# Two small loads move from SyncE's queue to ScalarE's, ahead of a two-stack transformer kernel

## The chip, the cores and the metric
The kernel runs on one core of a Trainium2 chip. The metric is the device time of one launch in microseconds (us), the median of several runs. The profile is of one further execution; its times count from the start of its span.

## What is computed
The reference runs x, 512 tokens of 1024 float32 values, through two layers of one kind (differential attention, a gated unit and dilated attention side by side, each fed by one wide projection, merged through gates) and then two of another kind (four kinds of attention side by side and a gated feed-forward part). Each layer of the first kind begins with an RMS norm, and that is all the change is near:
```python
def rmsnorm(t, g):
    tf = t.astype(jnp.float32)
    y = tf * lax.rsqrt(jnp.mean(tf * tf, axis=-1, keepdims=True) + EPS)
    return (y * g.astype(jnp.float32)).astype(t.dtype)

def hybrid_layer(x, ...):
    h = rmsnorm(x, norm_g)
    proj = jnp.einsum('bsd,dc->bsc', h, w_in)
    ...
```
So nothing of a layer can be computed before x, the factors norm_g and the first columns of w_in are on the chip.

## The kernel before
**Products.** Every weight matrix is cut into units of 128 x 1024 values (512 KB). SyncE loads them in the order of use into a ring of raw buffers. ScalarE rounds each to a high part (w_hi, line 1285), and VectorE subtracts to get the low part (w_lo, line 1302). TensorE multiplies in three products, high by high, low by high and high by low (lines 667 to 669). Each engine has its own program, written out by hand in order, and the engines meet at semaphores. A later load waits until TensorE has finished with the unit whose buffer it takes (`unit_done`, in `load`).

**The start.** x comes in four blocks of 128 tokens, 512 KB each. For a block, ScalarE makes the sum of squares and from it one factor per token (`rms`, lines 622 to 624; its results are in `small`). VectorE multiplies the block by this factor and by the gain row (`rms_scale`, line 630, into hn). TensorE transposes hn with the help of an identity matrix (line 601). ScalarE and VectorE take high and low part of the transposed block (h_hi line 609, h_lo line 615). Then the first products begin.

**The gain row.** norm_g is needed on every partition as a row of 1024 values, and it is in memory with 8 values on each of 128 partitions (`colp[:, 0:P1_SUBLN]`, 4 KB in all). VectorE waits for the identity (line 2000, `ident_loaded`) and then for these factors (line 1316, `norm_loaded`), and multiplies the one by the other in two halves of 128 x 512 (`gain_diagonal`, line 1318, gain_diag). TensorE multiplies each half by a matrix of ones, which sums over the partitions (`gain_sums`, line 1312), and VectorE copies the sums to gain_row (line 1913). The identity is 128 x 128 values, 64 KB (`const[:, 0:P]`).

**TensorE until then.** Its program begins with two products of zeros, one of 512 and one of 256 columns (line 1340), which wait only for a VectorE memset. Behind them it waits for the identity and then for gain_diag:
```python
pe.wait_ge(zeros_ready, 1)
zero_products(1)
zero_products(1, SEQ // 2)
pe.wait_ge(ident_loaded, 16)
gain_sums(pe)
entry_transpose(pe, e, 0, hn[0], (0,))
zero_products(2)
v_block(0, 0)
```

**The order of work.** VectorE: gain_diag twice, gain_row's first half, hn of block 0, w_lo of unit 0, h_lo, the high part of unit 1 (line 1924), hn of block 1, w_lo of unit 1, gain_row's second half. ScalarE: a load of its function table (line 1628), the statistics of block 0, w_hi of unit 0, h_hi of block 0, the statistics of block 1, and so on. SyncE: the identity (line 1104), the factors (line 1105), then x's blocks (line 1107) and the first four weight units (line 1073) in turns, then the remaining parameters, tables and masks (lines 1112 to 1119), one after the other with no wait among them.

Of the kernel before, what the change touches and what calls it, by code (L numbers as in the profile page):

```python
# [37 lines left out]
P = 128  # L38
# [64 lines left out]
P1_NORM, P1_SUBLN, P1_LAM, P1_INIT, P1_KEEP = 0, 8, 9, 9 + 4 * HD, 10 + 4 * HD  # L103
# [52 lines left out]
def program(nc, x_in, pos_in, const_in, mask_in, swa_in, rope2_in, col_in, w_in, row1_in,  # L156
            row2_in, out):
    ctx = ExitStack()
    with ctx:
# [4 lines left out]
        def sb(name, shape, dt=F32, at=None):  # L164

            size = 4
            for s in shape[1:]:
                size *= s
            offset = top[0] if at is None else at
            addr[name] = offset  # L170
            if at is None:
                top[0] += (size + 31) // 32 * 32
            return nc.alloc_sbuf_tensor_at(name, shape, dt, offset=offset)
# [3 lines left out]
        def sem(name):  # L177
            made = ctx.enter_context(nc.semaphore(name))
            names[made.num] = name
            return made  # L180
# [42 lines left out]
        const = sb("const", [P, C_KEEP])  # L223
        colp = sb("colp", [P, COLS])
# [106 lines left out]
        ident_loaded = sem("ident_loaded")  # L331
        params_loaded = sem("params_loaded")
        cols_loaded = sem("cols_loaded")
        norm_loaded = sem("norm_loaded")
# [298 lines left out]
        def ln_stat(act, st, i, tb):  # L633

            act.wait_ge(ln_centre, NB * i + tb + 1)
            st.wait(st(nc.scalar.activation(junk[:, :], x[:, tb, :], ACT.Square, bias=small[:, 52 + tb:53 + tb],
                                            accum_out=small[:, 16 + tb:17 + tb])))
            st.wait(st(nc.scalar.activation(small[:, 20 + tb:21 + tb], small[:, 16 + tb:17 + tb], ACT.Ln,
                                            scale=1.0 / D, bias=LN_EPS)))
            nc.scalar.activation(small[:, 20 + tb:21 + tb], small[:, 20 + tb:21 + tb], ACT.Exp, scale=-0.5) \  # L640
              .then_inc(ln_ready, 1)

        def ln_gain(st, i, tb):

            return st(nc.vector.scalar_tensor_tensor(out=hn[tb][:, :], in0=x[:, tb, :], scalar=small[:, 52 + tb:53 + tb],
                                                     in1=ln_row[:, 0:D], op0=ALU.add, op1=ALU.mult))

        def ln_scale(dve, i, tb, cols=slice(0, D)):

            dve.wait_ge(ln_ready, NB * i + tb + 1)  # L650
            return nc.vector.scalar_tensor_tensor(out=x[:, tb, cols], in0=hn[tb][:, cols], scalar=small[:, 20 + tb:21 + tb],
                                                  in1=ln_row[:, D:2 * D][:, cols], op0=ALU.mult, op1=ALU.add)
# [407 lines left out]
        def sync_program(sp):  # L1060
# [40 lines left out]
                sp.wait_ge(unit_done, first_unit(DEPTH + layer) + B2_END + i + 1)  # L1101
                sp.dma_start(raw_of(n), w_in[stored_at(n), :, :]).then_inc(last_loaded[i], 16)

            sp.dma_start(const[:, 0:P], const_in[:, 0:P]).then_inc(ident_loaded, 16)
            sp.dma_start(colp[:, 0:P1_SUBLN], col_in[0, :, 0:P1_SUBLN]).then_inc(norm_loaded, 16)
            for tb in range(NB):
                sp.dma_start(x[:, tb, :], x_in[tb * P:(tb + 1) * P, :]).then_inc(x_loaded[tb], 16)
                if tb < 2:
# [160 lines left out]
        def cast_to(act, n):  # L1269


            for u in range(cast_units[0], min(n, UNITS - 1) + 1):
                if u in EXTRA:
                    e, i = EXTRA[u]
                    if EXTRA_TURN[u] == extras_cast[0]:
                        cast_extra(act, e)
                elif u in TURN:
                    act.wait_ge(raw_loaded[TURN[u] % RAW], 16 * loaded_parts(u))
                    if u in STEP_OF and STEP_OF[u][2] == 1:
                        act.wait_ge(pair_sums, 4 * (PAIR_STEPS * STEP_OF[u][0] + STEP_OF[u][1]) + 2)  # L1280
                    if u in KR_UNITS:
                        nc.scalar.activation(by_tile(hi_of(u))[:, :, kr_high], by_tile(raw_of(u))[:, :, kr_high], ACT.Copy) \
                          .then_inc(hi_cast, 1)
                    else:
                        nc.scalar.activation(hi_of(u), raw_of(u), ACT.Copy).then_inc(hi_cast, 1)  # L1285
                cast_units[0] = u + 1

        def split_to(dve, n):


            for u in range(split_units[0], min(n, UNITS - 1) + 1):
                if u in EXTRA:
                    if EXTRA_TURN[u] == extras_split[0]:
                        split_extra(dve, *EXTRA[u])
                elif u in TURN:
                    dve.wait_ge(hi_cast, TURN[u] + 1)
                    if u in KR_UNITS:
                        high = by_tile(hi_of(u))
                        nc.vector.tensor_tensor(high[:, :, kr_low], by_tile(raw_of(u))[:, :, kr_high], high[:, :, kr_high].bitcast(F32),
                                                ALU.subtract).then_inc(split_done, 1)  # L1300
                    else:
                        nc.vector.tensor_tensor(lo_of(u), raw_of(u), hi_of(u).bitcast(F32), ALU.subtract) \  # L1302
                          .then_inc(split_done, 1)
                split_units[0] = u + 1
# [1696 lines left out]
        def last_down(dve, layer):  # L3001


            at, n_end = Counts(names, DEPTH + layer), first_unit(DEPTH + layer + 1)

            def one(tb, between=None):
                for c in range(2):
                    residual_sum(dve, at(tok_ready, 2 * (NB - 1) + tb + c), n_end - LAST_UNITS // 2 * (1 - c), c, 1.0, tb, True,
                                 LAST_BANKS[c])
                    if between and c == 0:  # L3010
                        between(tb - 1)
                centre(dve, at(tok_out, 2 * NB + 2 * tb + 2), tb)
                dve.wait_ge(ln_centre, NB * LN2[layer] + tb + 1)
            return one
# [423 lines left out]
        with nc.Block() as block:  # L3438
            @block.sync
            def _(sp):  # L3440
                sync_program(sp)

            @block.tensor
            def _(pe):
                for layer in range(DEPTH):
                    tensor_block1(pe, layer)
                for layer in range(DEPTH):
                    tensor_block2(pe, layer)

            @block.scalar  # L3450
            def _(act):
                st = Steps(act, act_step)
                for layer in range(DEPTH):
                    scalar_block1(act, st, layer)
                for layer in range(DEPTH):
                    scalar_block2(act, st, layer)
                nc.scalar.preload_act_table_set("natural_log_exp_and_others")
                cast_to(act, UNITS - 1)
                for tb in range(NB):
                    ln_stat(act, st, LN2[-1], tb)  # L3460
                act.wait_ge(final_ready, NB + 1)
                act.dma_start(out[(NB - 1) * P:NB * P, SEQ:D], x[:, NB - 1, SEQ:D]).then_inc(stored, 16)

            @block.vector
            def _(dve):
                st = Steps(dve, dve_step)
                for layer in range(DEPTH):
                    vector_block1(dve, st, layer)
                for layer in range(DEPTH):
                    vector_block2(dve, st, layer)  # L3470
                split_to(dve, UNITS - 1)
                i, residual = LN2[-1], last_down(dve, DEPTH - 1)
                dve.wait_ge(ln_rows_loaded, 16 * (i + 1))
                gained = {}

                def finish(tb):
                    st.wait(gained[tb])
                    ln_scale(dve, i, tb).then_inc(final_ready, 1)

                for tb in range(NB):  # L3480
                    residual(tb, finish if tb else None)
                    gained[tb] = ln_gain(st, i, tb)
                st.wait(gained[NB - 1])
                for c in range(2):
                    ln_scale(dve, i, NB - 1, slice(c * SEQ, (c + 1) * SEQ)).then_inc(final_ready, 1)
# [165 lines left out]
```

## Time and profile before
| | us |
|---|---|
| median of 3 runs (2294.7 to 2295.55) | 2294.81 |
| the profiled execution | 2294.94 |
| its span | 2293.1 |
| TensorE busy | 2279.9 |
| VectorE busy | 1618.4 |
| ScalarE busy | 1046.4 |

The clock that TensorE was granted over the span was 0.999 of full speed. PE is TensorE's matmuls and PEld its weight loads, DVE is VectorE, ACT is ScalarE, SP is SyncE; SPq and ACTq are the issues of transfers on these engines. A row of an operation gives output and inputs by the names in the program, their shapes, and, in square brackets, how long the engine stood idle before it and what it waited for.

### The profile page before, as it was taken

What the parts mean: (1) busy time and instruction counts of PE and PEld (TensorE: products, weight loads), DVE (VectorE), ACT (ScalarE), POOL (GpSimd) and SP (SyncE); (2) the same over time, 40 slices, a digit from 0 to 9 for tenths busy, and PEclk for the clock granted to TensorE, in tenths of its full rate; (3) what the DMA queues carried; (4) which work ended last, traced back from release to release, by engine and by line L of the source; (5) the groups of instructions that cost most, each with busy time, mean ns of one, the idle gap of its engine ahead of it and who ended that gap; (6) DMA issues with size and microseconds to landing.
All of it is one profiled execution on the core that took longest, in us unless ns stands there. A gap on an engine that the chain in (4) does not pass through costs nothing.

```text
span 2293.1 us, 31916 instructions
## 1 busy us (share of the span) xinstructions
PE 2279.9 (99%) x12048; PEld 1892.9 (83%) x12048; DVE 1618.4 (71%) x3021; ACT 1046.4 (46%) x1972; POOL 0.2 (0%) x4
## 2 busy tenths in 40 slices
PE   9999999999999999999999999999999999999998
PEld 7888888998888888998877788888887768888887
DVE  6788768775578777875677768567567786668565
ACT  5456544443446554443567533223246764223222
POOL 0000000000000000000000000000000000000000
PEclk9999999999999999999999999999999999999999
DMA  5343333343343333334231242424303113422422
GB/s 177 105 111 105 98 78 115 107 143 101 129 118 106 106 95 109 102 102 156 69 89 56 66 140 74 138 65 129 129 29 102 47 47 104 146 92 81 134 65 96
DMA packets 81624, 232.67 MB, mean 101 GB/s; under 512 B 16000, under 2 KB 16896, under 8 KB 80704
## 3 DMA queue, kind: packets, MB, share of 16 engines
q1 hardware_dynamic: 81328, 230.37, 32.6%
q8 instruction: 97, 1.59, 0.3%
q14 instruction: 55, 0.45, 0.1%
q10 hardware_dynamic: 144, 0.26, 0.0%
HBM read 208.96 MB, written 4.20 MB: 93 GB/s over the span
## 4 chain that ended last, share of the span: by engine, by line
PE 98%; DVE 1%; ACT 0%; issue 0%; DMA 0%; DVEq 0%; SPq 0%
PE bank L667 24%; PE bank L669 23%; PE bank L668 23%; PE bank L1593 3%; PE bank L1592 3%; PE bank L1591 3%; PE bank L2676 2%; PE bank L2677 2%; PE bank L2678 2%; PE bank L1454 2%; PE bank L1438 1%; PE bank L2459 1%; PE bank L2491 1%; PE bank L2475 1%; PE bank L601 1%; PE bank L1427 1%
## 5 line engine op out<-in xcount | busy, mean ns | idle before, releaser
L667 PE MATMUL bank<-h_hi,w_hi 128*128 128x512 f32 x1680 | 666.1, 396 | 0.2
L669 PE MATMUL bank<-h_lo,w_hi 128*128 128x512 f32 x1680 | 655.0, 390 | 0.0
L668 PE MATMUL bank<-h_hi,w_lo 128*128 128x512 f32 x1680 | 654.8, 390 | 0.0
L1302 DVE TENSOR_TENSOR w_lo<-raw_w,w_hi 128x1024 fp32r<-128x1024 f32 x294 | 355.8, 1221 | 79.3 <-ACT w_hi L1285 76.9
L1285 ACT ACTIVATE w_hi<-raw_w 128x1024 fp32r<-128x1024 f32 x293 | 307.6, 1054 | 180.1 <-DMA raw_w<-w_dram 172.3
L667 PEld LDWEIGHTS bank<-h_hi,w_hi 128*128 128x128 f32 x1680 | 315.7, 188 | 69.8 <-issue 8.6
L669 PEld LDWEIGHTS bank<-h_lo,w_hi 128*128 128x128 f32 x1680 | 315.4, 188 | 67.4
L668 PEld LDWEIGHTS bank<-h_hi,w_lo 128*128 128x128 f32 x1680 | 315.9, 188 | 60.3
L2923 ACT ACTIVATE nrm<-bank 128x512 f32<-128x512 f32 x44 | 26.3, 598 | 286.4 <-PE bank L669 286.4
L3337 DVE TENSOR_TENSOR ytmp<-nrm,bank 128x512 f32<-128x512 f32 x26 | 17.9, 687 | 117.0 <-PE bank L669 116.9
L1757 ACT ACTIVATE prob<-prob,small 128x128 f32<-128x128 f32 (+3 forms) x128 | 70.8, 556 | 61.5 <-DVE small L893 61.5
L2676 PE MATMUL bank<-seven_hi,y_hi 128*128 128x512 f32 x252 | 98.0, 389 | 0.0
L2677 PE MATMUL bank<-seven_hi,y_lo 128*128 128x512 f32 x252 | 98.0, 389 | 0.0
L1845 ACT ACTIVATE ext<-bank 128x256 f32<-128x256 f32 x72 | 27.6, 383 | 130.9 <-PE bank L1593 130.1
L3337 DVE TENSOR_TENSOR y_raw<-nrm,bank 128x512 f32<-128x512 f32 x18 | 12.4, 687 | 91.5 <-PE bank L669 91.5
L3405 DVE SCALAR_TENSOR_TENSOR x<-x,bank 128x512 f32<-128x512 f32 x84 | 54.8, 682 | 20.7 <-PE bank L2678 20.7
L1772 ACT ACTIVATE pT<-bank 128x384 f32<-128x384 f32 (+3 forms) x84 | 36.8, 470 | 61.4 <-PE bank L1438 61.3
L893 DVE CUSTOM_DVE_ANT_0 prob<-bank,causal 128x128 f32<-128x128 f32 (+3 forms) x96 | 43.2, 487 | 29.3 <-PE bank L1427 20.3
L2937 ACT ACTIVATE seven_hi<-sum_raw 128x512 fp32r<-128x512 f32 x54 | 31.2, 621 | 56.4 <-PE bank L2678 56.4
L667 PE MATMUL bank<-act_hi,proj_hi 128*128 128x512 f32 x144 | 56.3, 391 | 0.0
L668 PE MATMUL bank<-act_hi,proj_lo 128*128 128x512 f32 x144 | 56.2, 391 | 0.0
L2678 PE MATMUL bank<-down_lo,y_hi 128*128 128x512 f32 x144 | 56.0, 389 | 0.0
(456 smaller groups left out, 4576.4 us busy)
## 6 DMA issues: line engine op xcount, KB each, us to landing
raw_w<-w_dram SPq DMA_DIRECT2D x276, 512.0 KB, 3.6
down_raw<-w_dram SPq DMA_DIRECT2D x36, 512.0 KB, 4.5
raw_w<-w_dram SPq DMA_DIRECT2D x36, 256.0 KB, 3.0
proj_raw<-w_dram SPq DMA_DIRECT2D x36, 256.0 KB, 2.9
extra_raw<-w_dram SPq DMA_DIRECT2D x10, 512.0 KB, 4.7
x<-x_dram SPq DMA_DIRECT2D x8, 512.0 KB, 6.4
k_lo<-k_lo SPq DMA_DIRECT2D x32, 128.0 KB, 2.3
ln_row<-row_dram SPq DMA_DIRECT2D x4, 1024.0 KB, 6.6
```

The source lines that it names most:

```text
L667: nc.tensor.matmul(dst, lh, rh, start=start, stop=False)
L668: nc.tensor.matmul(dst, ll, rh, start=False, stop=False)
L669: return nc.tensor.matmul(dst, lh, rl, start=False, stop=stop)
L1285: nc.scalar.activation(hi_of(u), raw_of(u), ACT.Copy).then_inc(hi_cast, 1)
L1302: nc.vector.tensor_tensor(lo_of(u), raw_of(u), hi_of(u).bitcast(F32), ALU.subtract) \
L1591: nc.tensor.matmul(to, high[:, w], m_hi, start=begin, stop=False, skip_group_check=True)
L1592: nc.tensor.matmul(to, low[:, w], m_hi, start=False, stop=False, skip_group_check=True)
L1593: made = nc.tensor.matmul(to, high[:, w], m_lo, start=False, stop=k == 3, skip_group_check=True)
L1757: nc.scalar.activation(prob[m][:, own], prob[m][:, own], ACT.Exp, scale=-1.0, bias=small[:, 24 + 2 * qb + m:25 + 2 * qb + m], accum_out=sm ...
L2676: nc.tensor.matmul(bank[t][:, :], y_hi[:, p, a, y], high, start=begin, stop=False, skip_group_check=True)
L2677: nc.tensor.matmul(bank[t][:, :], y_lo[:, p, a, y], high, start=False, stop=False, skip_group_check=True)
L2678: made = nc.tensor.matmul(bank[t][:, :], y_hi[:, p, a, y], low, start=False, stop=p == PAIRS - 1, skip_group_check=True)
```

## The change
The two first issues of SyncE's program are taken out. ScalarE's program begins with them, in the other order: the factors first, then the identity. SyncE's program now begins with x's first block. The semaphores that the two transfers raise, and who waits for them, stay as they are.
```diff
@@ sync_program
-            sp.dma_start(const[:, 0:P], const_in[:, 0:P]).then_inc(ident_loaded, 16)
-            sp.dma_start(colp[:, 0:P1_SUBLN], col_in[0, :, 0:P1_SUBLN]).then_inc(norm_loaded, 16)
             for tb in range(NB):
                 sp.dma_start(x[:, tb, :], x_in[tb * P:(tb + 1) * P, :]).then_inc(x_loaded[tb], 16)
                 if tb < 2:
@@ the program of ScalarE
                 st = Steps(act, act_step)
+                act.dma_start(colp[:, 0:P1_SUBLN], col_in[0, :, 0:P1_SUBLN]).then_inc(norm_loaded, 16)
+                act.dma_start(const[:, 0:P], const_in[:, 0:P]).then_inc(ident_loaded, 16)
                 for layer in range(DEPTH):
                     scalar_block1(act, st, layer)
```

## Rows read from the trace of the kernel before
**Rows 1.** The page: busy time of TensorE, and the chain by engine.
```profile
PE 2279.9 (99%) x12048; PEld 1892.9 (83%) x12048; DVE 1618.4 (71%) x3021; ACT 1046.4 (46%) x1972; POOL 0.2 (0%) x4
...
PE 98%; DVE 1%; ACT 0%; issue 0%; DMA 0%; DVEq 0%; SPq 0%
```
**Rows 2.** Waits of TensorE after 30 us: total us, times, longest.
```profile
PE bank L2475 <- DVE pn L3091: 1.5, 4, 0.5
PE bank L2400 <- DVE sq_lo L3234: 1.4, 2, 0.7
```
**Rows 3.** The chain that ended last, first 13 us: start us, us, what.
```profile
0.73 0.40 SPq L1104
...
1.18 2.41 DMA colp<-col_dram
...
3.69 0.70 DVE gain_diag L1318
...
4.53 2.06 PE bank L1312 x2
...
6.62 0.70 DVE gain_row L1913
...
7.34 0.76 DVE hn L630
...
12.92 0.50 PE bank L667
```
**Rows 4.** The timeline, SyncE's queue: start us, us, line, transfer.
```profile
1.64 0.43 SPq L1107 DMA_DIRECT2D x<-x_dram  x1
...
7.87 0.43 SPq L1116 DMA_DIRECT2D rowp<-row_dram  x1
...
23.29 2.15 SPq L1073 DMA_DIRECT2D raw_w<-w_dram  x2
```
**Rows 5.** The timeline, ScalarE, first 7 us.
```profile
0.73 1.28 ACT L1628 ACT_TABLE_LOAD   x1 [0.73 <-PEq L3645]
5.58 1.06 ACT L622 ACTIVATE junk<-x 128x1024 f32<-128x1024 f32 x1 [3.56 <-DMA x<-x_dram]
...
6.99 0.20 ACT L624 ACTIVATE small<-small 128x1 f32<-128x1 f32 x1
```
**Rows 6.** The timeline, TensorE and its weight loads, first 9 us.
```profile
1.45 2.93 PE L1340 MATMUL bank<-ytmp 128*128 128x512 f32 x4 [1.45 <-DVE ytmp L1998]
2.46 0.34 PEld L1340 LDWEIGHTS bank<-ytmp 128*128 128x128 f32 x1 [0.52 <-issue]
...
3.31 0.34 PEld L1340 LDWEIGHTS bank<-ytmp 128*128 128x128 f32 x1 [0.52 <-issue]
...
4.53 3.24 PE L1312 MATMUL bank<-gain_diag,const 128*128 128x512 f32 x4 [0.16 <-DVE gain_diag L1318]
...
8.15 0.66 PE L601 MATMUL bank<-const,hn 128*128 128x128 f32 x4 [0.38 <-DVE hn L630]
```
**Rows 7.** DMA issues of the start: count, KB, us from issue to landing.
```profile
const<-const_dram SPq DMA_DIRECT2D x1, 64.0 KB, 1.8
...
rowp<-row_dram SPq DMA_DIRECT2D x1, 1024.0 KB, 12.1
...
x<-x_dram SPq DMA_DIRECT2D x1, 512.0 KB, 3.9
```
**Rows 8.** Windows (window, length, engines, PEclk, DMA share, GB/s), and the DMA page of 4.7:5.2.
```profile
2.60:3.40 0.80, 0.80 (x3) 0.28 (x2) 0.00 (x0) 0.00 (x0) 0.00 (x0) 1.00 0.60 119
...
DMA packets 54, 0.20 MB, mean 401 GB/s; under 512 B 5, under 2 KB 5, under 8 KB 54
```
**Rows 9.** ScalarE's only issue before, at the end, and both queues' landings.
```profile
2290.67 0.37 ACTq L3462 DMA_DIRECT2D out_dram<-x  x1
...
out_dram<-x SPq DMA_DIRECT2D x1, 256.0 KB, 2.0
out_dram<-x ACTq DMA_DIRECT2D x1, 256.0 KB, 2.1
```

## The prediction
> **What bounds the kernel now.** I read the page's busy shares and its chain first, since a change to loads at the start can only act through whatever sets the end. TensorE is busy for 2279.9 of 2293.1 us, and the chain that ended last is TensorE for 98% [rows 1]. So 13.2 us are left in which TensorE does nothing. The second view is where they lie. Behind the first 30 us the two largest of its waits come to 1.5 + 1.4 = 2.9 us in all, on VectorE and not on a DMA [rows 2]. At the start it waits 1.45, 0.16 and 0.38 us [rows 6], and the last matmul is followed by the norm and the store of the last block. A load at the start therefore has one way to the time: it moves the moment at which TensorE begins its unbroken work, and the rest slides along with it.
>
> That moment is read from the chain of the first 13 us [rows 3]. It runs: SyncE's issue of the identity; then the factors' transfer (colp), 2.41 us, landed at 3.59; VectorE's gain_diag from 3.69; TensorE's two gain products from 4.53; the copy to gain_row at 6.62; hn at 7.34; the transposes of it at 8.15 [rows 6]; and so on over h_hi and the second block's statistics to the product at 12.92. The first block of x is not in it. It landed for the statistics at 5.58, and the last of them began at 6.99 and ended at 7.19 [rows 5], while gain_row ended at 7.32. So **x's first block has 0.13 us of slack, and the factors have none.** This is the reading on which all below rests: the change brings earlier what was not late, and puts what was late beside a large transfer.
>
> **The change, part by part.** *SyncE* loses two issues, and its third began at 1.64, where the first had begun at 0.73 [rows 3, 4]. Every load behind them moves up by 1.64 - 0.73 = 0.91 us: four blocks of x, four weight units, the parameters and masks. None of these is waited for on the chain, and SyncE next issues at 23.29, when it has had to wait for TensorE to free a unit [rows 4], so its lead ends there. Worth of the lead by itself: x's statistics would start at 5.58 - 0.91 = 4.67 and end at 6.28; hn waits for gain_row anyhow: 0. ScalarE's cast of unit 0 would come 0.91 earlier too, but the w_lo that reads it is queued on VectorE behind hn, which ends at 8.10: 0 again. Should the factors come earlier, this slack is what lets them gain.
>
> *ScalarE* gets the two issues ahead of its table load. They cost about 0.4 us each on SyncE [rows 3] and 0.37 us for ScalarE's own issue at the end [rows 9]. The load of 1.28 us moves from 0.73 to about 1.6 and ends at 2.9; the statistics want it at 4.67 at the earliest. The cover is 1.8 us: 0. Even two issues of 1 us each would be hidden. The last store from ScalarE is the only use that queue had before [rows 9]; it landed in 2.1 us where SyncE's landed in 2.0, so a first use costs no more than 0.1 us, and I take 0.
>
> *The factors and the identity.* They now start at 0.73 and about 1.18, in the other order. VectorE waits for both, TensorE's gain products for the gain_diag made from them. With nothing beside them: the factors at 0.73 + 2.41 = 3.14, the identity at 1.18 + 1.8 = 2.98 [rows 3, 7]. Both are in 0.45 us sooner than the 3.59 of now. That gain is not all usable. TensorE fills the wait with two zero products; their weight loads stand at 1.44, 2.46 and 3.31 [rows 6], 0.85 us apart for a pass of 512 columns, and the last product has 256 columns, so two passes of 0.43 from 3.31: TensorE is free at 4.17. The first half of gain_diag, at 0.45 us earlier, would end at 3.69 - 0.45 + 0.70 = 3.94, before that. The gain product starts at 4.53 now; the floor is thus 4.53 - 4.17 = **0.36 us of gain at most**.
>
> But there is something beside them. The first x block is now issued at the same moment, 512 KB in 128 rows of 4 KB, and in the trace a small transfer never ran beside such a one from its start. What it would cost I bound from the rate: from 4.7 to 5.2 us the engines moved 401 GB/s with 54 packets [rows 8], 25 GB/s for each of 16, so 0.16 us for a packet of 4 KB. Each of the two small transfers has 128 / 16 = 8 packets on each engine. If every one waits for one of x's, that is 8 x 0.16 = 1.28 us, and the factors land at 3.14 + 1.28 = 4.42, 0.83 us later than now. If none waits, the gain of 0.36 stands. Between these I go by how busy the engines were while x's first packets came in now: from 2.6 to 3.4 us their busy share was 0.60 [rows 8]. So about 0.6 x 1.28 = 0.77 us, the factors at 3.91, and the chain **0.32 us later**. The far bound is x's own block, 3.9 us from issue to landing with a unit behind it [rows 7]: if the identity, issued at 1.18, took as long, it would land at 5.1, and cost 1.5 us.
>
> The Trainium skill, DMA: Bandwidth & Descriptors, section "Issuing engines are not separate DMA queues", says that transfers issued from ScalarE and SyncE run on the same 16 DMA engines and interleave, and that using several issuers saves only the sequencer's issue time. By that rule the 0.45 us of issue time are the whole gain, and the interleaving is the price. The trace before shows no moment with both queues at work at the start.
>
> **The sum.** 0 (SyncE's lead) + 0 (ScalarE's issues) + 0.32 (factors and identity) = +0.3 us. The profiled execution took 2294.94 us, of which 2293.1 are the span and 1.84 lie around it, and would become 2295.26. It stands 0.13 above the median of the three runs, 2294.81, so my number is 2294.81 + 0.32 = 2295.1 us.
>
> **The rivals.** *A, the small transfers slip through.* If the engines serve the second queue's packets without delay, the chain gains up to 0.36 us: 2294.45. For it: 32-byte and 512-byte rows take little room, and the share of 0.60 shows engines idle while x's first packets were due [rows 8]. Against it: both queues start at the same moment. Chance 0.33.
>
> *B, a whole burst goes first.* Each engine sends all 8 of x's packets before it turns to the other queue. The factors land at 4.42, and the identity may end with x at up to 5.1: a loss of 0.8 to 1.5 us, 2295.6 to 2296.3. For it: once x's packets flow the engines are full, at 401 GB/s [rows 8]. The Trainium skill, same page, section "Queues, rings and completion order", says that an engine drains a packet of about 9 to 17 descriptors from one queue's ring before it turns to the next; by that rule x's 8 would go as one. Chance 0.15.
>
> *C, the second queue starves, and the kernel is clearly slower.* If the engines served SyncE's backlog first, the identity would land when that backlog does. Its last large load was issued at 7.87 and landed 12.1 us later [rows 4, 7], at 20 us. The change would move that to 19.1, and the gain chain from 3.6 to 19.1: +15.5 us, 2310.3. It decides once the identity lands later than 3.59 + 4.6 = 8.2 us. Against it: at the end of the kernel ScalarE's 256 KB went out in 2.1 us, though with nothing beside it [rows 9]. Chance 0.02.
>
> *D, nothing moves.* What is won in issue time and lost to interleaving cancels to within 0.1 us: 2294.8. Chance 0.10. That the change does not do what it says is hardly possible here: a moved issue is a moved issue.
>
> **How the numbers follow.** My own case, a loss of 0.1 to 0.8 us, has 0.39; the last 0.01 is for an earlier start that also frees TensorE by more than I can find. A measurement of this kernel can tell a change of about 0.2%, that is 4.6 us. All cases but C and that last one lie within 1.5 us of no change, 0.07%. Faster is 0.01, the same 0.97, slower 0.02. The range takes the floor of 0.36 below and the far bound of 1.5 above, and half of the 0.85 us by which the three runs differ on each side: 2294.81 - 0.36 - 0.43 = 2294.0 and 2294.81 + 1.51 + 0.43 = 2296.8.
>
> **What would show it.** In the profile after, SyncE's first issue, at 0.73, is of x, and ScalarE has two issues ahead of a table load near 1.6. The statistics on ScalarE start near 4.7 instead of 5.58, and end with some 1 us of slack before hn. I expect gain_diag to start near 4.0 (3.69 now), the first gain product near 4.85, and the product at 12.92 to come near 13.2. If gain_diag starts at 3.3 and the first gain product at 4.2, A was right; at 4.5 or later, B; a wait for DMA of over 8 us ahead of gain_diag would be C. The forecast is wrong in its reason if ScalarE's statistics, and not gain_row, turn out to be what hn waits for, or if the products after 13 us do not move by what the start moved.

## The result, and the profile after

The changed kernel took **2298.07 us** (median of 21 runs, 2296.82 to 2299.51). The kernel before took 2294.88 us in 21 runs of the same sessions (2294.32 to 2295.55). The ratio is 1.0013, with a 95% interval of 1.0008 to 1.0019. It is slower by 3.2 us or 0.14%: under the 0.2% that I had called the limit, which many runs can evidently go below, and beyond the upper end of my range (2296.8). I had forecast 2295.1.

The profiled execution took 2298.2 us, its span is 2296.4 us, 3.3 more than before. The page, as in [rows 1]:
```profile
PE 2280.7 (99%) x12048; PEld 1892.7 (82%) x12048; DVE 1618.5 (70%) x3021; ACT 1046.8 (46%) x1972; POOL 0.2 (0%) x4
...
PE 97%; DVE 1%; ACT 1%; DMA 0%; issue 0%; DVEq 0%; ACTq 0%
```
The work is the same, and the loss is a wait. The chain of the first 16 us, which answers to [rows 3] (line numbers are 2 lower from line 1106 on):
```profile
0.74 0.40 ACTq L3451
...
1.17 5.20 DMA const<-const_dram
...
6.39 0.70 DVE gain_diag L1316
...
7.23 3.75 PE bank L1310 x4
...
13.69 0.75 DVE hn L630
14.44 1.15 DVE w_lo L1300
...
15.63 0.50 PE bank L667
```
The identity, issued at 1.17, landed 5.20 us later. gain_diag starts at 6.39 (3.69 before), the first gain product at 7.23 (4.53), and the product that stood at 12.92 now stands at 15.63: 2.70 us later, all of it behind that one transfer. ScalarE, which had waited for x, as in [rows 5]:
```profile
0.74 0.40 ACTq L3451 DMA_DIRECT2D colp<-col_dram  x1
...
1.17 0.45 ACTq L3452 DMA_DIRECT2D const<-const_dram  x1
...
1.65 1.28 ACT L1626 ACT_TABLE_LOAD   x1 [1.65 <-PEq L3645]
...
4.74 1.06 ACT L622 ACTIVATE junk<-x 128x1024 f32<-128x1024 f32 x1 [1.81 <-DMA x<-x_dram]
```
x came 0.84 us earlier and its statistics were done by 6.4; hn then waited for gain_row until 10.04. The table load moved and cost nothing. Both as forecast.

What the engines moved meanwhile is in the DMA page of two stretches, 2.5 to 4.4 and 4.4 to 5.9 us. q1 is SyncE's queue and q10 ScalarE's; the columns are packets, MB, share of the 16 engines.
```profile
q1 hardware_dynamic: 161, 0.59, 82.3%
q10 hardware_dynamic: 150, 0.01, 4.6%
...
q1 hardware_dynamic: 151, 0.55, 90.0%
q10 hardware_dynamic: 138, 0.06, 14.3%
```
In 3.4 us the engines took 0.59 + 0.55 = 1.14 MB of SyncE's queue, which is some 278 rows of 4 KB, 17 for each engine, and 150 + 138 = 288 packets of ScalarE's, 18 for each. The 288 are all there are: 128 rows and 16 closing packets for each of the two transfers. Totals over 16 engines could also come from bursts that alternate. Shorter stretches speak against that, 3.5 to 3.7 and 4.7 to 4.9 us, in which an engine makes about one turn:
```profile
q1 hardware_dynamic: 16, 0.07, 81.5%
q10 hardware_dynamic: 16, 0.00, 4.5%
...
q1 hardware_dynamic: 17, 0.07, 84.5%
q10 hardware_dynamic: 17, 0.01, 14.3%
```
In the trace's record of single packets, 108 of the factors' 128 are followed within 6 ns by the start of a 4 KB packet, where chance would give about 40%. So the queues take turns packet by packet, one large for one small, and the identity's packets stand behind the factors' in their queue. That is the main reading; the experiments test it. (The records do not name the engine of a packet, so the order on a single engine is inferred from this.)

### The profile page after: what moved, and what is told of

Same layout as the page of the kernel before. It is cut to its first block, busy times and chain, and to the rows that moved or that the text cites. A ratio compares the mean times of both kernels' runs of the same rounds, so it can differ in the third digit from the quotient of the medians.

```text
span 2296.4 us, 31916 instructions
## 1 busy us (share of the span) xinstructions
PE 2280.7 (99%) x12048; PEld 1892.7 (82%) x12048; DVE 1618.5 (70%) x3021; ACT 1046.8 (46%) x1972; POOL 0.2 (0%) x4
## 4 chain that ended last, share of the span: by engine, by line
PE 97%; DVE 1%; ACT 1%; DMA 0%; issue 0%; DVEq 0%; ACTq 0%
PE bank L667 23%; PE bank L669 23%; PE bank L668 23%; PE bank L1591 3%; PE bank L1590 3%; PE bank L1589 3%; PE bank L2676 2%; PE bank L2674 2%; PE bank L2675 2%; PE bank L1452 2%; PE bank L1436 1%; PE bank L2457 1%; PE bank L2489 1%; PE bank L2473 1%; PE bank L601 1%; PE bank L1425 1%
```

## The experiments

The theory, **S (in series)**: a packet of the second queue waits for one 4 KB packet of the first, some 0.19 us a turn, and 16 turns go one after the other, not 8 as I had counted. The rivals: a price of the second queue by itself, whatever else is moved (Q, or F where it is a fixed delay per transfer); x's burst going first (B); only the kind of transfer mattering (N). The times stand against the kernel before in the same session: 2295.1 us for the first four kernels, 2295.24 for the next four, 2295.3 for the last. The edits are shown against the changed kernel in 1, 6, 7 and 10, against the kernel before in 2, 3, 4 and 8, and against run 3 in 11; [...] and lines of three dots stand for what is left out.

**1. The order on ScalarE's queue turned round.**
```diff
-                act.dma_start(colp[...], col_in[...]).then_inc(norm_loaded, 16)
                 act.dma_start(const[...], const_in[...]).then_inc(ident_loaded, 16)
+                act.dma_start(colp[...], col_in[...]).then_inc(norm_loaded, 16)
```


> Both transfers stay on ScalarE's queue, the identity first, the factors second. Theory S (in series): while SyncE's queue has rows of 4 KB to move, each engine takes one of them for each small packet of ScalarE's queue, and the two small transfers have 8 + 8 packets on an engine, one behind the other; the order does not matter, gain_diag starts at 6.4 us as in the changed kernel (0.3 either way), time 2298 us. Rival F (fixed delay): each transfer on the second queue is late by an amount of its own, whatever is queued ahead; then the identity, now first, lands near 4.9 and the factors near 6.4 again, but with the factors alone slow (the identity lands as fast as x's share allows, 4.0): gain_diag at 5 to 5.5, 2297.0.

Measured: 2298.61 us, ratio 1.0014 (1.0006 to 1.0023). Its DMA issues:
```profile
const<-const_dram ACTq DMA_DIRECT2D x1, 64.0 KB, 4.2
colp<-col_dram ACTq DMA_DIRECT2D x1, 4.0 KB, 5.1
```
In the changed kernel it was the other way, the factors 4.2 and the identity 5.2 us. Whichever is second is late, whether its rows have 32 or 512 bytes; gain_diag started at 6.36. S holds, F and N do not.

This run shows a second loss beside the first. gain_diag, gain product (7.20) and hn (10.01) stood as in the changed kernel, and yet the product that stood at 12.92 came at 16.04, 0.41 later than there. TensorE's zero products behind the transposes, first in the changed kernel, then in this run:
```profile
11.35 1.88 PE L1338 MATMUL bank<-ytmp 128*128 128x512 f32 x4
```
```profile
11.72 2.68 PE L1338 MATMUL bank<-ytmp 128*128 128x512 f32 x4
```
The same work took 0.8 us more. It is taken up in the last section.

**2 and 3. Only one of the two on ScalarE's queue,** the other first on SyncE's, ahead of x.
```diff
-            sp.dma_start(colp[...], col_in[...]).then_inc(norm_loaded, 16)
...
                 st = Steps(act, act_step)
+                act.dma_start(colp[...], col_in[...]).then_inc(norm_loaded, 16)
```
and in the other kernel the same with the identity:
```diff
-            sp.dma_start(const[...], const_in[...]).then_inc(ident_loaded, 16)
...
                 st = Steps(act, act_step)
+                act.dma_start(const[...], const_in[...]).then_inc(ident_loaded, 16)
```


> Only the factors are on ScalarE's queue; SyncE begins with the identity, then x. Theory S: 8 packets an engine in place of 16, beside x from its start: 2.6 + 8 x 0.2 = 4.2, landed 4.8, gain_diag at 4.9 (3.69 before), 1.2 us later than before, 2296.1 us. Rival F (a fixed price of the second queue, whatever the count): as the changed kernel, gain_diag at 6, 2297.5 or more. Rival N (only the identity's large rows suffer): gain_diag at 3.3, 2294.5.

> Only the identity is on ScalarE's queue; SyncE begins with the factors, then x. Theory S: again 8 packets an engine, from some 2.6 us on, 0.2 us each: landed 4.8, gain_diag at 4.9, 2296.1 us. Rival F: gain_diag at 6, 2297.5 or more. Rival N: the large rows suffer, so as late as in the changed kernel, gain_diag 6.4, 2298.

Measured: 2295.44 us (ratio 1.0002, 0.9993 to 1.001) with the factors moved, 2295.18 us (1.0001, 0.9992 to 1.0009) with the identity moved. Both expectations of S were wrong by far. The DMA issues of the first, then of the second:
```profile
const<-const_dram SPq DMA_DIRECT2D x1, 64.0 KB, 1.9
colp<-col_dram ACTq DMA_DIRECT2D x1, 4.0 KB, 2.1
```
```profile
const<-const_dram ACTq DMA_DIRECT2D x1, 64.0 KB, 2.0
colp<-col_dram SPq DMA_DIRECT2D x1, 4.0 KB, 1.8
```
gain_diag started at 2.91 and 2.78, 0.8 to 0.9 us earlier than before. The DMA page of the second from 1.7 to 2.4 us says why:
```profile
q1 hardware_dynamic: 152, 0.04, 52.0%
q10 hardware_dynamic: 144, 0.07, 36.1%
```
x is now issued at 1.18, one slot of 0.45 us behind, and only 8 of its rows fall into this stretch; ScalarE's 144 packets are through before x's stream begins. I had taken the 2.6 us at which the second queue began in the changed kernel for a property of the queue, but it belongs to x's being there first. What decides is the start: **the second queue costs nothing for a transfer that has left the engines before the bulk arrives.** In both kernels the first gain product stood at 4.17, exactly the floor that the prediction had read from the zero products.

**4. Both on SyncE's queue, the factors first.**
```diff
-            sp.dma_start(const[...], const_in[...]).then_inc(ident_loaded, 16)
             sp.dma_start(colp[...], col_in[...]).then_inc(norm_loaded, 16)
+            sp.dma_start(const[...], const_in[...]).then_inc(ident_loaded, 16)
```


> Both on SyncE's queue as in the kernel before, the factors first. No second queue. The transfer with the longer way of the two (factors, 2.41 us from issue to landing) starts 0.45 us earlier: 0.73 + 2.41 = 3.14, identity 1.18 + 1.8 = 2.98. gain_diag at 3.2, the gain product at TensorE's floor of 4.17: 0.36 us gained, 2294.5 us. If instead the 2.41 us of the factors came from their place behind the identity or beside x, the identity in that place is as late: gain_diag at 3.7, 2294.9, no change.

Measured: 2295.29 us, ratio 1.0001 (0.9992 to 1.001), no change. The gain chain did gain, gain_diag at 3.24 and the gain product at the floor. But this time x landed at 5.96 (5.58 before), and hn waited for it:
```profile
7.69 0.75 DVE L630 SCALAR_TENSOR_TENSOR hn<-x,small,gain_row 128x512 f32<-128x512 f32 x1 [1.17 <-ACT small L624]
```
The 0.13 us of slack that I had read for x is also the most that the gain chain can bring by itself.

**5. The kernel before, a second profile.**

> The kernel before once more, for a second profile of it. The changed kernel's products start 2.70 us late at the first gain product and 3.33 us late from the 65th us on. If the other 0.6 is scatter of the landing of a weight unit near 40 us, this profile's products near 65 us may stand up to 0.6 us later than in the first profile with the start unmoved. If it belongs to the change, both profiles agree to 0.1 us.

Measured: one execution of 2296.18 us. Its start:
```profile
3.06 1.29 DVE L1318 TENSOR_TENSOR gain_diag<-const,colp 128x512 f32<-128x512 f32 x2 [1.53 <-DMA colp<-col_dram]
...
7.37 0.75 DVE L630 SCALAR_TENSOR_TENSOR hn<-x,small,gain_row 128x512 f32<-128x512 f32 x1 [0.56 <-ACT small L624]
```
gain_diag at 3.06 instead of 3.69, hn at 7.37 instead of 7.34. The landing of the factors scatters by 0.6 us, and x's statistics, just behind it, cover that. Which of the two is late differs from run to run, and the time hardly does.

**6. Both on ScalarE's queue, x held until they have landed.**
```diff
+            sp.wait_ge(norm_loaded, 16)
+            sp.wait_ge(ident_loaded, 16)
             for tb in range(NB):
```


> The changed kernel, but SyncE waits for both small transfers before it issues x. Theory S (the small transfers are slow only because bulk shares the engines): the identity lands near 1.17 + 1.8 = 3.0, gain_diag at 3.1, gain product at TensorE's floor of 4.17. x is issued at 3.1, lands 3.9 us later at 7.0, statistics to 8.6, hn at 8.65 where it was 7.34: 1.3 us later than before, 2296.4 us. Rival Q (ScalarE's queue is slow by itself): the identity lands at 6.4 even so, x at 10.3, hn near 12: over 4 us later, 2299.5.

Measured: 2298.42 us, ratio 1.0013 (1.0004 to 1.0022). Its DMA issues, and ScalarE's wait for x:
```profile
const<-const_dram ACTq DMA_DIRECT2D x1, 64.0 KB, 2.3
colp<-col_dram ACTq DMA_DIRECT2D x1, 4.0 KB, 1.7
```
```profile
7.33 1.06 ACT L622 ACTIVATE junk<-x 128x1024 f32<-128x1024 f32 x1 [4.43 <-DMA x<-x_dram]
```
2.3 us in place of 5.2 for the same instruction on the same queue: Q falls, the bulk alone made it slow. x cost the 1.3 us foreseen and some more (hn at 9.06, 1.7 late). The remaining loss is another one, told further below.

**7. Both on ScalarE's queue, the bulk behind x's first block held.**
```diff
             for tb in range(NB):
                 sp.dma_start(x[:, tb, :], x_in[tb * P:(tb + 1) * P, :]).then_inc(x_loaded[tb], 16)
+                if tb == 0:
+                    sp.wait_ge(norm_loaded, 16)
+                    sp.wait_ge(ident_loaded, 16)
```


> The changed kernel, but after x's first block SyncE waits for both small transfers before it issues anything more. Theory S: x's 8 packets on each engine go in turns with the factors' 8, the identity's 8 then have the engines to themselves: 2.6 + 8 x 0.2 + 0.3 = 4.5, landed near 4.8; gain_diag at 4.9, 1.2 us later than before, 2296.2 us, unless the held weight units become late. Rival B (x's whole burst goes first, the rest after it): the same landing or earlier, and the 32-byte packets all start behind the last 4 KB packet. Rival Q: 6.4 as in the changed kernel.

Measured: 2296.8 us, ratio 1.0008 (0.9999 to 1.0017). Its DMA issues:
```profile
const<-const_dram ACTq DMA_DIRECT2D x1, 64.0 KB, 3.6
colp<-col_dram ACTq DMA_DIRECT2D x1, 4.0 KB, 3.8
```
gain_diag started at 4.79 (4.9 expected by S). The factors, which share the engines with x, are about as slow as ever (3.8). The identity behind them, which now has the engines to itself, lands 1.6 us sooner after its issue. gain_diag is 1.6 us earlier than in the changed kernel: so much of the loss comes from the weight unit and x's second block, behind x's first (1.3 us against the second profile of the changed kernel, run 9). The time itself is not clear of no change, and it is not a clean measure either: the product that stood at 12.92 came at 14.48, and what it waited for was no longer the gain chain but the held weight unit, which landed at 9.06.

**8. Both on SyncE's queue, right behind x's first block.**
```diff
-            sp.dma_start(const[...], const_in[...]).then_inc(ident_loaded, 16)
-            sp.dma_start(colp[...], col_in[...]).then_inc(norm_loaded, 16)
             for tb in range(NB):
                 sp.dma_start(x[:, tb, :], x_in[tb * P:(tb + 1) * P, :]).then_inc(x_loaded[tb], 16)
+                if tb == 0:
+                    sp.dma_start(colp[...], col_in[...]).then_inc(norm_loaded, 16)
+                    sp.dma_start(const[...], const_in[...]).then_inc(ident_loaded, 16)
```


> Both small transfers on SyncE's queue, right behind x's first block. Theory S: no taking of turns in one queue, so the 16 small packets of an engine follow x's 8 in a row: x from 1.8 to 3.2 us or so, the small ones until 3.9, landed at 4.5; gain_diag at 4.6, 0.9 us later than before, 2296.0 us, and earlier than in the changed kernel though issued 0.9 us later. Rival (what matters is only that x is ahead): as late as in the changed kernel, 6.4, 2298.

Measured: 2297.24 us, ratio 1.0007 (0.9998 to 1.0016). The identity's issue and landing:
```profile
const<-const_dram SPq DMA_DIRECT2D x1, 64.0 KB, 3.3
```
Issued at 1.64, landed at 4.9, gain_diag at 4.93 (4.6 expected; 6.39 in the changed kernel). Issued half a microsecond later, in the same queue as x and behind it, the identity comes 1.4 us sooner than from a queue of its own (1.2 us against run 9). From 3.3 to 3.7 us, all in SyncE's queue:
```profile
DMA packets 248, 0.11 MB, mean 268 GB/s; under 512 B 151, under 2 KB 233, under 8 KB 248
```
233 small packets and 15 of 4 KB: in one queue the small ones went almost in a row, although the weight unit had been issued at 2.11. The time is 2.0 us above the kernel before, where the changed kernel had 3.2, and its interval touches no change.

**9. The changed kernel, a second profile.**

> The changed kernel once more, for a second profile. If the start alone carries the loss, the identity lands again near 6.3 us and the first gain product starts 2.6 to 2.8 us later than in the first profile of the kernel before; what comes on top by the 65th us may differ from the 0.6 of the first profile by as much again.

Measured: one execution of 2297.98 us, the identity 4.9 us from issue to landing, gain_diag at 6.08, the gain product at 6.92, 2.39 us later than in [rows 6]. The start's loss repeats, at 2.4 to 2.7 us.

**10. One small issue put ahead of x.**
```diff
+            sp.dma_start(const[:, C_INV:C_KEEP], const_in[:, C_INV:C_KEEP]).then_inc(inv_loaded, 16)
             for tb in range(NB):
```
(and taken out further down)

> The changed kernel, with one issue put ahead of x on SyncE's queue: the 4 KB of the rope constants, which come later otherwise. x is issued at 1.18, beside the identity on ScalarE's queue; the factors, issued at 0.74, are one slot ahead of it. Theory S, with the first slot deciding: the factors land free at 2.8, the identity takes turns with x for its 8 packets: 2.3 to 4.4, landed at 4.9. gain_diag at 4.9, 1.2 us later than before, 2296.3 us. Rival (one slot ahead frees the whole second queue): both landed by 3.3, gain product at the floor of 4.17, 2295.1.

Measured: 2297.79 us, ratio 1.001 (1.0001 to 1.0019). Its DMA issues:
```profile
const<-const_dram ACTq DMA_DIRECT2D x1, 64.0 KB, 4.2
colp<-col_dram ACTq DMA_DIRECT2D x1, 4.0 KB, 1.9
```
The factors, one slot ahead of x, are free at 1.9 us; the identity, issued in the same slot as x, pays 4.2. The two prices stand side by side in one run. gain_diag started at 5.39, 0.5 later than expected: beside x, 8 small packets cost more than the 1.6 us that I had allowed.

**11. The zero product of 256 columns left out,** with only the identity moved.
```diff
                 zero_products(1)
-                zero_products(1, SEQ // 2)
                 pe.wait_ge(ident_loaded, 16)
```


> The kernel with only the identity on ScalarE's queue, and without the zero product of 256 columns on TensorE (line 1340 runs once before the gain products), which leaves nothing out of the result. gain_diag was at 2.78 there, its first half ready at 3.46, and TensorE was busy with zeros until 4.17. Now the gain product can start at 3.5, gain_row ends at 6.15, and hn waits for x's statistics, which ended at 6.55: hn at 6.6 where it was 6.85. 0.25 us less than with the identity moved alone, 0.75 less than before at the start: 2294.4 to 2294.9. If the shorter run of zeros leaves TensorE at its slower rate for longer, the gain products end no earlier and nothing is won.

Measured: 2295.26 us, ratio 1.0 (0.9991 to 1.0009). TensorE's gain products in the timeline, first of this kernel, then of run 3, which keeps the zero product:
```profile
3.67 3.75 PE L1311 MATMUL bank<-gain_diag,const 128*128 128x512 f32 x4
```
```profile
4.17 2.79 PE L1311 MATMUL bank<-gain_diag,const 128*128 128x512 f32 x4
```
The gain products started 0.5 us earlier and took 1 us longer. hn started at 6.70 where it had been at 6.85. It is the last case of the expectation: little is won (the last section has more on the slower passes). The products from 15 to 50 us stood 0.67 us earlier than before, in the two profiles with the identity alone moved 0.49 and 0.77.

**12. Only the identity moved, once more.**

> The kernel with only the identity on ScalarE's queue once more, for a second set of times and a second profile. It started 0.37 to 0.49 us early and yet had 2295.18 us against 2295.1. If the start's gain is real and the rest scatter, 2294.7 (0.3 either way). If something later takes it back each time, 2295.2 again and products near 65 us no earlier than in the second profile of the kernel before.

Measured: 2295.14 us, ratio 0.9999 (0.9991 to 1.0008). hn started at 6.46, 0.88 us earlier than in the kernel before, and still nothing is left of it at the end. Where it goes is read 35 us later. TensorE's waits between 30 and 80 us in this run:
```profile
PE bank L667 <- DVE sz L2049: 0.9, 1, 0.9
PE bank L667 <- DVE w_lo L1301: 0.2, 1, 0.2
```
And the high part of a weight unit on ScalarE, with its wait for the landing, first in this run, then in the two profiles of the kernel before, then in the changed kernel:
```profile
41.74 1.06 ACT L1284 ACTIVATE w_hi<-raw_w 128x1024 fp32r<-128x1024 f32 x1 [1.72 <-DMA raw_w<-w_dram]
```
```profile
40.95 1.06 ACT L1285 ACTIVATE w_hi<-raw_w 128x1024 fp32r<-128x1024 f32 x1 [0.28 <-DMA raw_w<-w_dram]
```
```profile
41.55 1.06 ACT L1285 ACTIVATE w_hi<-raw_w 128x1024 fp32r<-128x1024 f32 x1 [0.77 <-DMA raw_w<-w_dram]
```
```profile
44.30 1.06 ACT L1283 ACTIVATE w_hi<-raw_w 128x1024 fp32r<-128x1024 f32 x1 [0.83 <-DMA raw_w<-w_dram]
```
From this landing on VectorE has a chain of some 20 us (norm of the gate, rotation angles, low parts), from 46 to 66 us with hardly a gap, and TensorE catches up with it at 53 and at 65 us. So there is a **second joint**: what follows is set by the later of the start and that landing, which is issued when TensorE frees a unit and came 0.3 to 1.7 us after ScalarE was ready for it in these four. The moment at which ScalarE starts this high part says where the products behind 65 us stand. By how much each is later than in the first profile of the kernel before, in us, products matched one by one:

| | products of 15 to 50 | this high part | products of 66 to 70 |
|---|---|---|---|
| before, second profile | 0.00 | 0.60 | 0.60 |
| changed, first and second | 2.72, 2.38 | 3.35, 2.89 | 3.33, 2.92 |
| run 1 | 3.49 | 3.59 | 3.59 |
| identity moved, runs 3 and 12 | -0.49, -0.77 | 0.03, 0.79 | 0.03, 0.80 |

In the other profiles, too, the last two agree to 0.02 us. So the joint adds 0.1 to 0.6 us to a late start (1.5 in run 7) and takes an early one back, by 0.5 and 1.6 us here. In the first profile of the kernel before its wait was the shortest of the four, yet that execution, 2294.94 us, lies near its kernel's median, while the second, 2296.18, lies above all 26 timed runs of its session (2296.08 at most); another 0.6 us of its lateness comes behind 70 us, which was not followed up.

## Why the prediction was wrong

**Right.** *The path.* TensorE's unbroken work begins behind the chain factors, gain_diag, gain products, gain_row, hn, and the rest slides with it: 2.70 us at the first gain product, 2.71 at the product of 12.92. *What is not on it.* SyncE's lead (x 0.84 us earlier, worth 0), ScalarE's issues ahead of the table load (0), the first use of ScalarE's queue (2.0 and 2.1 us from issue to landing in runs 2 and 3, where SyncE's had 1.8 and 1.9). *TensorE's floor* of 4.17 came out to the last digit in four kernels. *The sign.* The change loses, by interleaving with x.

**Wrong: the term "8 x 0.16 = 1.28 us, the factors and the identity", and the 0.6 that I put on it.** I took +0.32 us; it was +2.70. Three things in it failed.
- *The two small transfers are in series.* I let each wait for 8 of x's packets and took the later of the two. They share a queue, so an engine has 16 turns to make (18 with the closing packets): 18 x 0.19 = 3.4 us, from 2.5 to 5.9, where I had 1.28 (a turn is also 0.19 and not 0.16 us). Runs 1, 7 and 10 show this.
- *The bulk does not end with x's block.* The turns go on against the weight unit and x's second block; my bounds had counted x's 8 packets only. Run 7 takes these away and has 1.3 to 1.6 us back.
- *The engines' share of 0.6* was read while x's stream was starting up in the kernel before. In the changed kernel the share of SyncE's queue was 82% and 90%. Idle engines were hardly a discount.

The far bound, x's own 3.9 us, was no bound either, since nothing had ever taken turns with x. I had the right mechanism and no row for its size; such a term wants the number of packets ahead in the own queue times the turns, and not a likeness.

**Rivals.** A (slip through) is what happens when one transfer moves and x is one issue behind, but not in this change. B (a burst of x first) is refuted by the counts, 17 large against 18 small packets on an engine, and one for one also within 0.2 us. My own sign for B, gain_diag at 4.5 or later, was met all the same (6.39); it could not tell B from what happened. D (nothing moves) did not come. The Trainium skill, DMA: Bandwidth & Descriptors, section "Queues, rings and completion order", has an engine drain a packet of about 9 to 17 descriptors before it turns to the next queue; here the turns were single rows of 4 KB, as the trace counts packets. Its section "Issuing engines are not separate DMA queues" says that transfers of the two issuers run on the same engines and interleave, and that agrees. C (starvation) did not come, though its idea, that the backlog counts and not only x, held in part.

**The rest of the loss.** 3.2 us between the medians against 2.4 to 2.7 at the start. In its two profiles the second joint adds 0.6 and 0.5, so my sign that the products after 13 us move by what the start moved held only up to 50 us. It adds as much in the second profile of the kernel before, but nothing in the first, whose time is the typical one. Run 1 shows another candidate: hn stood as in the changed kernel, and behind TensorE's slower passes the products were 0.4 us later than there by the one of 12.92 and 0.8 later from 15 to 50 us. How the median's rest divides between the two was not settled.

No version beat the kernel before by more than its measurement's spread. The ones with a start 0.4 to 0.9 us earlier had 2295.14 and 2295.18 against 2295.3 and 2295.1.

## What to carry to other kernels

A small transfer that work waits for should not start beside bulk on another queue: it pays one bulk packet for each of its own, and so does every small transfer behind it in its queue. Put it ahead of the bulk, on the same queue or one issue earlier on another; even right behind the first bulk block on the same queue it landed 1.2 to 1.4 us sooner here than from a queue of its own beside the bulk. And before shortening one arm of a start, look for the other arm (here 0.13 us behind) and for the next joint (here a landing near 41 us): a gain goes only as far as both allow.

## What was not expected of the hardware

- One issue slot of 0.45 us between a small transfer and the bulk decides between 2 us and over 4 us from issue to landing (1.9 against 4.2 us in run 10).
- TensorE's four passes of the gain products took 3.24 us in the kernel before, 3.75 in the changed one, 2.79 and 2.18 in the two profiles of one and the same kernel with the identity moved. The column PEclk reads 1.00 in all these stretches, as it does in [rows 8], but only part of that is a measurement. The trace's first record of a granted clock, of full speed, begins at 7.1 us in the kernel before, at 10.9 and 10.5 in the two profiles of the changed one, at 6.0 and 4.8 with the identity moved, and at 13.3 in run 1; ahead of it the column shows 1.00 for want of a record. Ahead of it a pass of 512 columns took 0.85 us (weight loads at 8.22 and 9.07 in the changed kernel), behind it 0.43 (at 11.78 and 12.21). That fits the lower of the two levels, 1.2 GHz against 2.4, but no record says so.
- So in run 1 the late start cost twice. The changed kernel and run 1 had TensorE idle for 2.86 and 2.83 us ahead of the gain products; the record of full speed began at 10.9 in the one and 13.3 in the other, and the transposes took 0.67 against 1.11 us. Both profiles of the changed kernel had the milder case; its other executions have no trace.
- In run 6 TensorE had nothing to do for 2.35 us while hn waited for x, and then the granted clock fell to its lower level, this time on record. The windows of 1 us at 9, 11 and 12 us (the last three columns are PEclk, the DMA share and GB/s):
```profile
9.00:10.00 1.00, 0.13 (x1) 0.13 (x2) 0.82 (x2) 0.90 (x1) 0.00 (x0) 1.00 1.04 418
11.00:12.00 1.00, 1.00 (x2) 0.34 (x1) 0.86 (x3) 1.00 (x2) 0.00 (x0) 0.50 0.97 389
12.00:13.00 1.00, 1.00 (x3) 0.35 (x2) 0.79 (x2) 0.70 (x4) 0.00 (x0) 0.50 1.01 414
```
  From full speed (2.4 GHz) to half (1.2 GHz). The first weight product took 1.11 us there, 0.54 in the kernel before, and the products, 1.7 us late at the transposes, were 2.6 us late by the one that had stood at 12.92. This, the 0.4 us by which hn was later than expected, and 0.5 us at the second joint are what run 6 lost beyond its expectation.
